# A third feed-forward stage computed in pairs of steps, with its keys' and values' work moved into four early steps

## The reference, cut to what matters

```python
def swiglu(x, w_gu, w_down):
    gate, up = jnp.split(x @ w_gu, 2, axis=-1)        # width 2816 each
    return (jax.nn.silu(gate) * up) @ w_down

x = x + 0.5 * swiglu(rms_norm(x, ffn1_norm[0]), ...)  # ffn0
...                                                   # delta-rule mixer, memory attention
x = x + 0.5 * swiglu(rms_norm(x, ffn2_norm[0]), ...)  # ffn1
ckr = rms_norm(x, kv_in_norm) @ w_dkv                 # 256 latent columns and 64 for the rotation
c_kv = rms_norm(ckr[..., :KV_LORA], kv_lat_norm)
k_rope = apply_rope(ckr[..., None, KV_LORA:], cos, sin)[:, :, 0]
k_nope, v_mla = jnp.split((c_kv @ w_ukv).reshape(b, s, B_HEADS, 256), [128], axis=-1)
x = x + 0.5 * swiglu(rms_norm(x, ffn1_norm[1]), ...)  # ffn2
...                                                   # attention over k_nope, k_rope, v_mla
x = x + 0.5 * swiglu(rms_norm(x, ffn2_norm[1]), ...)  # ffn3
...                                                   # hybrid layer, whose feed-forward is ffn4
```

## Time and profile before

| | |
|---|---|
| Median of three runs | 1297.39 us (1296.99 to 1298.51) |
| Profiled execution, its own time | 1295.02 us |
| Its span, first to last instruction | 1293.2 us |
| Mean granted TensorE clock | 0.999 |
| PE busy | 1275.6 us, 99% of the span |
| DVE, ACT, POOL busy | 949.1, 820.5 and 57.4 us |
| ffn1, from 376.0 to 553.7 us | 177.7 us |
| ffn2, from 553.7 to 761.1 us | 207.4 us |
| ffn3, from 831.0 to 1008.7 us | 177.7 us |

### The profile page before, as it was taken

The page is one execution under the profiler, slowest core; times in us unless marked ns, Lnnn a source line. Parts: engine busy times, 40 slices in busy tenths (PEclk is TensorE's granted clock), DMA queues, the critical chain, the costliest instruction groups (busy, mean ns, idle before and its releaser), DMA issues.

```text
span 1293.2 us, 17184 instructions
## 1 busy us (share of the span) xinstructions
PE 1275.6 (99%) x6940; PEld 1065.7 (82%) x6940; DVE 949.1 (73%) x1103; ACT 820.5 (63%) x1064; POOL 57.4 (4%) x85
## 2 busy tenths in 40 slices
PE   7999999999999999999999999999999999999998
PEld 6888888888988888888787888888888898788887
DVE  4888777877557888766354467678887799698885
ACT  7576658776556666684443466576666757766663
POOL 0000000000000000000000000000000100000000
PEclk9999999999999999999999999999999999999999
DMA  8987748888256677789887756776777883657772
GB/s 340 300 311 235 247 159 274 259 241 227 77 187 259 225 262 262 235 323 293 259 278 258 246 200 193 239 314 228 260 260 246 287 263 135 256 201 260 264 246 72
DMA packets 46686, 313.02 MB, mean 242 GB/s; under 512 B 5196, under 2 KB 7500, under 8 KB 9872
## 3 DMA queue, kind: packets, MB, share of 16 engines
q1 hardware_dynamic: 34080, 227.74, 46.3%
q0 software_dynamic: 11376, 81.54, 25.4%
q10 hardware_dynamic: 1152, 2.66, 0.6%
HBM read 310.85 MB, written 52.44 MB: 281 GB/s over the span
## 4 chain that ended last, share of the span: by engine, by line
PE 93%; ACT 3%; DVE 2%; DMA 1%; issue 1%; SPq 0%; ACTq 0%; DVEq 0%
PE ps L2841 24%; PE ps L2842 24%; PE ps L2843 24%; PE ps L2756 8%; PE ps L2992 1%; PE ps L2767 1%; PE ps L2882 1%; PE ps L2874 1%; PE ps L2887 1%; ACT w_hi_part L671 1%; DVE w_lo_part L1730 1%; PE ps L2897 1%; PE ps L549 1%; DMA arena<-in_tiles 1%; PE ps L551 1%; PE ps L550 1%
## 5 line engine op out<-in xcount | busy, mean ns | idle before, releaser
L1730 DVE TENSOR_TENSOR w_lo_part<-w_raw,w_hi_part 128x2048 fp32r<-128x2048 f32 (+2 forms) x184 | 416.3, 2267 | 121.5 <-ACT w_hi_part L671 121.1
L671 ACT ACTIVATE w_hi_part<-w_raw 128x2048 fp32r<-128x2048 f32 (+1 forms) x183 | 346.4, 1897 | 142.4 <-PE ps L2843 130.7
L2841 PE MATMUL ps<-w_hi_part,x_hi 128*128 128x512 f32 (+1 forms) x740 | 289.7, 391 | 0.8 <-DVE w_lo_part L1730 0.5
L2843 PE MATMUL ps<-w_hi_part,x_lo 128*128 128x512 f32 (+1 forms) x740 | 282.4, 382 | 0.0
L2842 PE MATMUL ps<-w_lo_part,x_hi 128*128 128x512 f32 (+1 forms) x740 | 281.4, 380 | 0.0
L2841 PE MATMUL ps<-w_hi_part,h_hi_part 128*128 128x512 f32 x464 | 186.0, 401 | 0.0
L2842 PE MATMUL ps<-w_lo_part,h_hi_part 128*128 128x512 f32 x464 | 181.2, 391 | 0.0
L2843 PE MATMUL ps<-w_hi_part,h_lo_part 128*128 128x512 f32 x464 | 181.2, 391 | 0.0
L671 ACT ACTIVATE w_hi_part<-arena 128x2048 fp32r<-128x2048 f32 x66 | 126.1, 1916 | 64.8 <-PE ps L2843 37.0
L1730 DVE TENSOR_TENSOR w_lo_part<-arena,w_hi_part 128x2048 fp32r<-128x2048 f32 x66 | 150.2, 2288 | 21.1 <-ACT w_hi_part L671 20.6
L2843 PEld LDWEIGHTS ps<-w_hi_part,x_lo 128*128 128x128 f32 x740 | 139.1, 188 | 27.5
(11 more groups left out here) (461 smaller groups left out, 1554.5 us busy)
## 6 DMA issues: line engine op xcount, KB each, us to landing
w_raw<-in_tiles SPq DMA_DIRECT2D x179, 1024.0 KB, 6.6
made_sums<-in_tiles POOLq DMA_DIRECT2D x48, 1024.0 KB, 9.1
arena<-made_sums SPq DMA_DIRECT2D x24, 1024.0 KB, 8.1
arena<-in_tiles POOLq DMA_DIRECT2D x18, 1024.0 KB, 10.2
arena<-in_tiles SPq DMA_DIRECT2D x9, 1024.0 KB, 6.8
mem_kv<-in_tiles POOLq DMA_DIRECT2D x6, 1024.0 KB, 10.5
w_raw<-in_tiles SPq DMA_DIRECT2D x3, 512.0 KB, 6.6
arena<-in_w_ukv POOLq DMA_DIRECT2D x1, 1536.0 KB, 13.9
```

Of the source, the lines that this page charges most:

```text
L671: nc.scalar.activation(WH[:, n % RING, 0:w], source(n), ACT.Copy).then_inc(S["w_hi"], 1)
L1730: nc.vector.tensor_tensor(WL[:, n % RING, 0:w], source(n), WH[:, n % RING, 0:w], ALU.subtract).then_inc(S["w_split"], 1)
L2841: nc.tensor.matmul(o, a_hi, w_hi, start=start, stop=False, skip_group_check=True)
L2843: return nc.tensor.matmul(o, a_lo, w_hi, start=False, stop=stop, skip_group_check=True)
```

## The change

ffn2 becomes a stage with pairs at steps 5, 7 and 9; steps 0 to 4 stay plain. The function `ffn` of ACT and DVE is gone, and `steps_of(name)` gives each stage's pairs. PE runs ffn2's first five steps in `late_steps`; ACT's and DVE's lists for ffn2 are `from_five`, those of the other stages `from_three`, unchanged. The kv work of steps 1 to 8 now stands in steps 1 to 4. DVE copies ffn2's activation blocks out of PSUM with the gain (`x_blocks`, eight instructions) and makes their sums in buffers of their own. `made_sums` holds 30 units instead of 24: POOL makes ffn2's six, five of them straight after ffn1's and the sixth between two t4 sums of ffn1; ffn3's and ffn4's are made partly at other times; each DMA still waits for the one before. SP loads the made sums; two of its waits are on the kv work (`kv_ps`). `length()`, in the mixer, always uses 64 columns where twelve matmuls had one.

Of the matmuls of 128x512, 36 are gone over the program: 764 products with x become 704 and 240 with the sums s become 288, each of three matmuls. DVE has nine more `w_lo`, three more t2 sums, one more `s_lo`, nine more sums of results and the eight copies of blocks; ACT nine more `w_hi`, one more `s_hi`, nine more copies of banks and one more table load; POOL 18 more DMAs (103 instructions instead of 85 in all), SP six more loads of made sums and three fewer of raw units.

The diff, cut to its core, shows in this order the stages, SP's loads, DVE's copies of blocks and the opening of its list, PE's first five steps, and POOL's list around ffn1.

```diff
-QUADS = ("ffn1", "ffn3", "ffn4")
-QUAD_STEPS = (3, 5, 7, 9)
+QUADS = ("ffn1", "ffn2", "ffn3", "ffn4")
+def steps_of(name):
+    return (5, 7, 9) if name == "ffn2" else (3, 5, 7, 9)
...
+                if n == unit_of["ffn2", "g1", 4]:
+                    sp.wait_ge(*made_all("ffn2"))
+                    sp.wait_ge(S["kv_ps"], 6)
+                    t_load("ffn2", 5, 0)
+                if n == unit_of["ffn2", "d", 3]:
+                    sp.wait_ge(S["kv_ps"], 11)
+                    t_load("ffn2", 5, 1)
+                    t_load("ffn2", 7, 0)
...
+                def x_blocks(half):
+                    for k in range(4):
+                        last = nc.vector.tensor_scalar(blocks[:, 2 * half:2 * half + 2, k, :], PS[:, half:4:2, k * P:(k + 1) * P],
+                                                       gain(name, 4 * half + k), None, ALU.mult)
...
+                def from_five():
+                    start()
+                    w_lo(at("g0", 1))
+                    first()
+                    x_blocks(0)
+                    x_blocks(1)
+                    plain_hidden(0, 0)
+                    plain_hidden(0, 1)
+                    w_lo(at("g1", 1))
...
+                def late_steps():
+                    opening(0)
+                    opening(1)
+                    quad_gate_up(1, 0)
+                    turn_pair(0)
+                    quad_gate_up(1, 1)
+                    pe.wait_ge(S["kv_sb"], 4)
+                    pe.wait_ge(S["x_blocks"], 2 * of_all(name) + 1)
+                    down_half(0, 0)
+                    kv_down(0)
+                    down_half(0, 1)
+                    turn_pair(1)
+                    kv_down(1)
+                    quad_gate_up(2, 0)
+                    kv_turn_rope()
+                    quad_gate_up(2, 1)
+                    kv_swap()
+                    down_half(1, 0)
+                    down_half(1, 1)
+                    turn_pair(2)
+                    kv_turn_latent()
+                    quad_gate_up(3, 0)
+                    kv_keys(0)
+                    quad_gate_up(3, 1)
+                    kv_keys(1)
+                    down_half(2, 0)
+                    kv_keys(2)
+                    down_half(2, 1)
+                    turn_pair(3)
+                    kv_values(0)
+                    quad_gate_up(4, 0, lambda: kv_values(1))
+                    kv_values(2)
+                    quad_gate_up(4, 1)
+                    pe.wait_ge(S["kv_sb"], 14)
+                    for s in steps:
+                        quad_of_steps(s)
...
-            t4_sums("ffn1")
-            pool.wait_ge(S["tile_used"], unit_of["ffn1", "m4", QUAD_STEPS[-1]] + 1)
+            paced(tile0["mem"] + 2)
+            makes("ffn2", 0, [tile0["mem"] + 3])
+            for i in range(1, 5):
+                make("ffn2", i)
+            t4_sum("ffn1", 3)
+            t4_sum("ffn1", 5)
+            make("ffn2", 5)
+            t4_sum("ffn1", 7)
+            make("ffn3", 0)
+            t4_sum("ffn1", 9)
+            pool.wait_ge(S["tile_used"], unit_of["ffn1", "m7", 9] + 1)
```

More of the change, by code:

```diff
@@ L262, in program @@
     bias_rows = nc.dram_tensor("bias_rows", [P * (ROW + 1)], f32, kind="Internal")
-    made = nc.dram_tensor("made_sums", [len(QUADS) * len(QUAD_STEPS), 2, P, TILE], f32, kind="Internal")
+    made = nc.dram_tensor("made_sums", [sum(len(steps_of(name)) for name in QUADS), 2, P, TILE], f32, kind="Internal")
     with ExitStack() as ctx:
@@ L918, in quad_ffn @@
             def quad_ffn(f, name, first):
+                steps = steps_of(name)
+                blocks = AF_OF.get(name, AF)
+                P5F, C11F, C12F = SNAPS_OF.get(name, (M1F, U2F, U3F))
                 def at(kind, s):
@@ L1996, in hidden @@
                     dve.wait_ge(S["sg_ready"], gates_to(f, s, tb))
-                    nc.vector.scalar_tensor_tensor(out=HFS[s % 2][:, tb, :], in0=up, scalar=RSV[:, tb:tb + 1], in1=sg,
+                    nc.vector.scalar_tensor_tensor(out=(HF if name == "ffn2" and s < steps[0] else halves[s % 2])[:, tb, :], in0=up, scalar=RSV[:, tb:tb + 1], in1=sg,
                                                    op0=ALU.mult, op1=ALU.mult).then_inc(S["h_raw"], 1)
@@ L2459, in _, with kv_scaled, kv_rope @@
-            ffn(2, "ffn2", lambda: after_ffn("ffn1", "ffn2"), lambda: inverse("ffn2"), kv_early)
+            def kv_scaled():
+                dve.wait_ge(S["lat_sd"], 1)
+                link(nc.vector.reciprocal(KRC, KSS))
+                for tb in range(TB):
+                    last = nc.vector.tensor_scalar(CK[:, tb, 0:2 * P], CK[:, tb, 0:2 * P], KRC[:, tb:tb + 1], None, ALU.mult)
+                last.then_inc(S["lat_f"], 1)
+            def kv_rope():
+                link(nc.vector.memset(KRZ, 0.0))
+                dve.wait_ge(S["rope_tab"], 2)
+                dve.wait_ge(S["kv_ps"], 4)
+                nc.vector.tensor_tensor(TURN, SIN, bank(7, SEQ), ALU.mult)
+                link(nc.vector.tensor_tensor(KR, KR, COS, ALU.mult))
+                nc.vector.tensor_tensor(KRZ[0:HALF, 0, :], KR[0:HALF, :], TURN[0:HALF, :], ALU.add)
+                nc.vector.tensor_tensor(KRZ[HALF:P, 1, :], KR[HALF:P, :], TURN[HALF:P, :], ALU.add).then_inc(S["rope_done"], 1)
@@ new lines, in lambdas @@
+            def lambdas():
+                nc.vector.tensor_tensor(G12[:, :], par("final_norm"), par("norm1_2"), ALU.mult)
+                nc.vector.tensor_scalar(SUBG[:, :], par("subln"), 1.0 - LAM_INIT, None, ALU.mult)
+                for j in range(2):
+                    last = nc.vector.tensor_tensor(LAMP[:, j, :], par("lam", 64 * j, 32), par("lam", 64 * j + 32, 32), ALU.mult)
+                link(last)
+                nc.vector.tensor_reduce(LAMS, LAMP[:, :, :], axis=AX.X, op=ALU.add).then_inc(S["lam_ready"], 1)
@@ L2462, in _, with lambda_out @@
+            def lambda_out():
+                dve.wait_ge(S["lam_exp"], 1)
+                link(nc.vector.tensor_tensor(NLAM, LAM2[:, 1:2], LAM2[:, 0:1], ALU.subtract))
+                nc.vector.tensor_scalar(NLAM, NLAM, -LAM_INIT, None, ALU.add).then_inc(S["lam_ready"], 1)
+            quad_ffn(2, "ffn2", lambda: after_ffn("ffn1", "ffn2"), lambda: inverse("ffn2"))
             after_ffn("ffn2", "bin")
@@ L3082, in quad_gate_up @@
                             last.then_inc(S["gu_ps"], 1)
+                        if tb == 0 and between:
+                            between()
                     last.then_inc(S["tile_used"], 1)
@@ L4128, in makes, with t4_sum, make @@
                         copy(name, i + 1)
[L4130 to L4134 removed]
+            def t4_sum(name, s):
+                split(name, "m6", s)
+                pool.dma_start(ta_of(name, s), stored(name, "g1", s), accum_op=ALU.add).then_inc(t4_added(name, s)[0], 16)
+            def make(name, i):
+                copy(name, i)
+                add(name, i)
             for s in PAIR_STEPS:
@@ L4155, in _ @@
             pool.wait_ge(S["bias_dma"], 16)
-            makes("ffn4", 3, [tile0["out1"] + 1, tile0["out1"] + 2])
-            t4_sums("ffn3")
+            makes("ffn4", 2, [tile0["out1"] + 1, tile0["out1"] + 2])
+            t4_sum("ffn3", 3)
+            t4_sum("ffn3", 5)
+            make("ffn4", 4)
+            t4_sum("ffn3", 7)
+            t4_sum("ffn3", 9)
             pool.dma_start(bass.AP(bias_rows, 0, [[ROW + 1, P], [1, ROW]]),
@@ L4167, in _ @@
             makes("ffn4", 5, [tile0["in2"] + 2, tile0["in2"] + 4, tile0["in2"] + 6])
-            t4_sums("ffn4")
+            for s in steps_of("ffn4"):
+                t4_sum("ffn4", s)
 def layout(a):
```

678 lines of the change are left out of this document (310 added, 368 removed).

## The result

The change made the kernel slower. Beside 1297.38 us for the kernel before it takes 1306.47 us (median of six runs each), a ratio of 1.0073 with a 95% interval of 1.0058 to 1.0087: some 9 us more, where 6.6 us less was forecast. The profiled execution has a span of 1305.1 us, 11.9 more than before.

What follows compares the result with a forecast made beforehand. PE was taken to bound the kernel, busy 1275.6 of 1293.2 us. Pairs saving 6.9 us and 0.3 us of waiting in ffn1's opening gave -6.6, so 1297.39 became 1290.8 us, range 1288.8 to 1294.8.

Steps and rivals of the forecast that it cites:

- The saving of the pairs: In ffn2, a pair takes 31.28 us against 33.58 for two plain steps: 2.30 us saved each, 6.90 for three.
- The kv work at nothing: In ffn2, moving the kv work from eight steps to four keeps its matmuls and was costed at nothing.
- rival (C): In ffn2's steps 1 to 4, packed kv work makes PE wait: ten pieces 1 us late, 1300.5 us; chance 0.05.
- (a): At ffn2's opening, DVE's eight block copies last about 2.5 us, leaving 0.9 us spare before PE needs the g1 split.
- The step on POOL's list: POOL's added sums delay no t4 sum; copies and adds during ffn1's opening cost PE 0.3 us.
- So one add costs 2.3 us of the spare time: Price from ffn3's opening, applied to ffn1's: two POOL transfers take 4.6 us of 5.4 us spare for g0 of step 2.
- the far bound: In ffn1's opening, two transfers at POOL's 4.0 us per MB cost 8.0 us, so PE would wait 2.6 us.
- rival (A): The burst at ffn1's opening makes PE wait: price 2.3 us, time 1292.8 us; chance 0.12.
- So no t4 sum goes out late.: In ffn1, POOL's six ffn2 sums leave about 13 us spare before the t4 sums are issued.
- Rival (B): t4 sums land late behind a copy or add: 16.1 us, PE waits 2.5 per pair, 7.5 in all, 1298.3 us; chance 0.05.
- POOL and SP have the same loads for each pair as in ffn1.: In ffn2's new pairs, the loads match those of ffn1's pairs and were costed at nothing.
- The signs that I had named for (A) and (B): (A): PE idle near 409 us, ended by a weight split behind an ACT waiting for a load; (B): idle ahead of m4.

Runs made afterwards that it cites:

- the last kernel: Changed kernel with POOL's sums moved out of the openings and all pairs, ffn4's sums 1 to 6 made before ffn4: ratio 0.9957 to the kernel before, 1289.2 us.
- the third experiment: Changed kernel with ffn2's six sums cut to 64 columns, one ffn3 sum behind ffn2's first t4 sum, ffn3's first at ffn2's opening: ratio 0.9978 to the kernel before.
- the kernel run twice: Changed kernel with POOL's sums moved out of the openings, two ffn4 sums left in ffn3's pairs: ratios 0.9963 and 0.9974 to the kernel before.
- the first experiment: Changed kernel with the ffn3 sum directly ahead of ffn2's first t4 sum made behind it, once landed: ratio 1.0031 to the kernel before, median 1299.69 us.

## Why the prediction was wrong

**The saving of the pairs** was right: 2.3 us for each of three, 6.9 us. ffn2 lasts 200.4 us in the last kernel where 207.4 - 6.9 = 200.5 was forecast, and its second pair takes 31.3 us (682.21 to 713.49). So was its counting at 0.228 us for a matmul.

**The kv work at nothing** was right; rival (C) fell. In the changed kernel PE has no wait and no gap from 563 to 688 us, through all of steps 1 to 4. Of the small terms (a) was under-sized: the eight copies of blocks took 3.2 us, 0.4 each, not 2.5 together, and the split behind them still came in time:

```profile
563.00:688.00 125.00, 125.00 (x556) 100.75 (x554) 78.67 (x101) 74.66 (x107) 7.71 (x11) 1.00 0.80 262
...
575.63 3.21 DVE L1964 TENSOR_SCALAR arena<-ps,params 128x256 f32<-128x256 f32 x8
```

**The step on POOL's list failed, in four terms.**

1. *"So one add costs 2.3 us of the spare time. About two transfers of POOL's fall into the burst of ffn1: 4.6 us, under 5.4."* The price came from an opening in which the add didn't meet that load at all. In the kernel before, ffn3's opening has its add here (POOL, then SP's queue), and it took 9.0 us to land:

```profile
832.73 0.82 POOL L4115 DMA_DIRECT2D made_sums<-in_tiles  x1 [6.34 <-DMA made_sums<-in_tiles]
...
846.56 0.33 SPq L610 DMA_DIRECT2D w_raw<-in_tiles  x1
```

It had landed at 841.7, and the load of g0 of step 2, the second row, was issued at 846.56. What I took for the price of an add on that load can only have been that of its tail on the loads ahead. In the changed kernel POOL's chain covered the burst from end to end with three transfers, and the load took 8.1 us longer, close to the 8.0 that I had worked out as the far bound, from POOL's queue as a whole, and then set aside in favour of the nearer row. The chain of copies and adds isn't a fixed number of transfers; it fills all the time it is given.

The spare time was wrong as well. By 5.4 us of it a load that is 8.1 late costs 2.7, and PE began 3.9 late. The rows are DVE and PE before, then DVE in the change:

```profile
404.56 0.87 DVE L1997 SCALAR_TENSOR_TENSOR arena<-ps,norm_rsv,arena 128x256 f32<-128x256 f32 x2
408.43 0.60 PE L2992 MATMUL ps<-consts,arena 128*128 128x128 f32 x4
...
408.79 2.29 DVE L1760 TENSOR_TENSOR w_lo_part<-w_raw,w_hi_part 128x2048 fp32r<-128x2048 f32 x1 [6.73 <-ACT w_hi_part L699]
411.00 0.87 DVE L2007 SCALAR_TENSOR_TENSOR arena<-ps,norm_rsv,arena 128x256 f32<-128x256 f32 x2
```

Behind the split of g0 of step 2 stands the hidden layer of step 1 on DVE's list, and PE turns it ahead of the product with g0. The split ended at 411.1, the hidden layer at 411.9, and the turn began at 411.92; I had counted to the product alone. The spare time was 8.1 - 3.9 = 4.2 us.

The Trainium skill ("DMA: Bandwidth & Descriptors", section "Queues, rings and completion order") says that each DMA engine takes turns between the queues that have work, packet by packet. This trace agrees: with POOL's queue almost never empty, SP's load took 16.8 us instead of 8.7.

2. *What a wait of PE costs.* I priced a late load at its lateness alone. Behind the waits of 3.9 and 6.6 us the granted clock was 0.50, which cost 2.4 and 2.6 us more. With it rival (A) would have been at 1290.5 + 3.9 + 2.4 + 2.2 for the small waits behind it, about 1299, above before, and its chance of 0.12 was far too low.

3. *"So no t4 sum goes out late."* True, and beside the point: I looked at when POOL issues a t4 sum, not at what lies ahead of it in its queue. ffn2's first t4 sum was issued on time at 671.0, half a microsecond behind an add that went out when its copy had landed, and took 19.3 us to land where 19.3 - 6.6 = 12.7 were to be had. Rival (B) had the mechanism, priced it at 16.1 us and 2.5 us of waiting, and I argued it away with ffn1's order, in which *"each t4 sum has its predecessor landed 13 us earlier"*. In ffn2 it had not. It alone made ffn2 slower, by 9.2 us with the clock.

4. *"POOL and SP have the same loads for each pair as in ffn1."* This left out ffn3's sums. In the kernel before they were made beside plain steps. The change takes six plain steps away, and a sum made in a pair brought the DMA share from 0.77 to 0.88 and then to 1.01 in the third experiment. Its price: two sums in ffn3's pairs cost 180.5 - 177.8 = 2.7 us in the kernel run twice, two in ffn2's 205.9 - 200.5 = 5.4 us in the third experiment's profiled execution, where the clock fell too; by the medians that kernel missed 6.9 - 2.9 = 4.0 us.

The range of 1288.8 to 1294.8 was made of the bounds of the wrong terms. The signs that I had named for (A) and (B) both came, (A)'s with the hidden layer behind the split in place of the split, and so did one of the tests for a wrong prediction: ffn2's first pair ran from 660.1 to 700.0 us, 39.9 instead of at most 32.5.

What stays open: why the clock fell behind some waits and not behind others. In the profiled executions, counted from start to start, it fell behind waits of 2.6, 2.8, 3.9, 6.0, 6.5 and 6.6 us, not behind those of 1.3, 2.2, 2.4, 3.0 and 3.7. I didn't test what decides between. The spread of runs (1303.3 to 1307.9 us for the changed kernel, 1298.7 to 1305.5 for the one with the transfers alone, 1289.3 to 1293.4 with two pairs) may go with it: of the first experiment's twelve runs the fastest, 1293.8 us, has a mean granted clock of 1.000 and the slowest, 1303.2, one of 0.997. That was not followed up.

## What to carry to other kernels

Before adding background transfers, lay them out in time against the foreground's loads, stage by stage: a chain in which each transfer waits for the last fills every gap, so ask which bursts it will cover, and take its price from a row where it did cover one. Look at what is queued ahead of a transfer, not only at when it is issued. Where an engine at 99% waits, add what it loses afterwards. And when a plan that saves work on the busy engine loses, try the same work with the transfers elsewhere before giving it up: here 9 us of loss became 5.4 us of gain by another order of one queue.
